# Reordering a sparse-attention stage: gates ahead of queries, alternating token tiles, and a delayed score step

## Chip, cores and metric

One core of a Trainium2 chip (trn2). The metric is the device time of one execution in microseconds (us); lower is better. The kernel is written by hand, one instruction stream for each engine: TensorE (PE, matmuls; PEld is its weight load), VectorE (DVE), ScalarE (ACT), GpSimd (POOL) and SyncE (SP, which only issues transfers). The streams meet at semaphores: `then_inc` raises one, `wait_ge` holds an engine's stream until it has reached a value.

## The reference

One layer of a decoder step for a prompt of 512 tokens and 8 samples of 8 new tokens (64 rows), all in float32, model width 1024:

```
h = rmsnorm(x);  z = h @ w_in           # hq hf hi hg | nq | kc vc ks vs kw vw | ngate | mgate
o_hg  = gated linear recurrence of 8 heads over hq, hf, hi, hg
o_nsa = g0 * compressed + g1 * selected + g2 * window     # 16 query heads, 4 kv heads of 64
u = sigmoid(mA) * o_hg + sigmoid(mB) * o_nsa;  x += rmsnorm(u @ w_out)
x += rmsnorm(conv_ffn(rmsnorm(x)))
```

The attention has three branches, each a softmax of its own, combined with a sigmoid gate per head and branch (`ngate`, 16 x 3 columns):

- compressed: means over blocks of 32 keys;
- selected: the 8 best blocks of 64 keys by the compressed probabilities (for the samples out of 4096 cached keys each, behind a page table); in the prompt of 512 tokens every causal block is selected;
- window: the last 512 keys.

The outputs are the new x, the new key and value rows of all branches, the window caches, the recurrence's states and the convolution's states.

## The kernel before

**Stages.** 0 to about 470 us: the norm of x and the recurrence, head by head, each with four products with 128 columns of `w_in`; beside it GpSimd gathers the compressed cache and DVE sums its blocks. To 547: the six key/value projections (blocks B_KV, units U_KV). To 571: transposes of the new keys (`kT`, units U_KT) and block means of the prompt (U_CM). To 635: eight query units (U_NQ), each 128 rows of queries for all 576 tokens. To 647: the gate unit (U_NG). To 857: the prompt's attention. To 1234: the samples' attention. Then merge gates, `w_out`, the FFN. The change touches 547 to 1234 us.

**Projection units** alternate between PSUM banks 0, 1 and 2, 3 (`2 * (u % 2)`); `banks_free(u)` waits until unit u - 2 has been copied away. Weights come in a ring of four slots on SP's queue (`weights(b)`, issued in order of b, L552). Before, the gate unit (L1936) runs behind the queries, with the tokens as the stationary operand: five token tiles by eight slices, 80 matmuls with 48 columns each. ScalarE takes the sigmoid of each tile (L958). Before `kT` is copied, ScalarE issues 13 transfers of new keys and values to the outputs (L940 to L944) on its own queue; its stream goes on to the copies of `kT` (L951, L952) behind them.

**The prompt's attention** is a list of 64 steps, `STEPS`, written out in this order: token tile i (0 to 3, 128 queries each), pair of kv heads gp, head r, branch br (selected or window). Step n does two heads (e = 0, 1) at once over (i + 1) * 128 keys. The engines work it in a pipeline:

- PE: `masked_scores(n)` (L1981, L1983) into banks 2 * (n % 2) and the next; transposes of the probabilities of step n - 2 (L2004); `values(n - 3)` (L1964, L1970).
- DVE: maximum of step n (L1425); reciprocal and scaling of head e = 0 of step n - 1 (L1430, L1433); copy of a transpose of step n - 2 (L1439); the output of every second step (L1411, L1412).
- ScalarE: exponential of step n (L979), copy of the other transpose (L989).
- GpSimd: scaling of head e = 1 (L747).

Every 16 steps, at the tile's end, the compressed branch of the next tile is done between the steps: `c_scores`, `c_exp`, `c_probs`, `c_transposes`, for all 16 heads of one tile. Ahead of its first scaling GpSimd issues 12 gathers of selected pages (`e_gather`, L736), which wait until the last projection unit is done, as their buffers lie in the weight ring.

**The samples' attention** is a loop of 96 steps. A sample has NC = 10 steps: c = 0 to 7 take four pages of 128 keys each, c = 8 the window of 512 keys, c = 9 the new rows. PE's step s:

- transposes the keys of step s: 8 transposes into banks 0 and 1 (L2091), one signal `ek_ok` behind both;
- transposes the probabilities of step m = s - LAG (L2099), LAG = 16, into banks 4 and 5 in turn;
- values of step m - 1 (`e_values`, L2055) into bank 6;
- scores of step s (L2116) from ScalarE's copy `kTs` of the transposed keys (L1034, both banks in one instruction);
- a piece of the block choice for the next sample: `e_c1` at c = 3, `e_c3` at 4, `e_c7` at 6, `e_c9` at 8.

DVE's step s waits for the scores of s, adds the block penalties (`penq`) and takes the maximum (L1525, L1528; L1530 to L1532 for the window); the block choice goes on in `e_c4`, `e_c6`, `e_c8` (L1465 to L1471), `e_c10` behind the scores of c = 4, 5, 7 and 9. ScalarE takes the exponentials of the last sample (`e_exp`, L1015) at c = 0 to 3, and DVE multiplies them with gate over sum (`e_scale`, L1483) at c = 4 to 6, before PE transposes them. Two merge gates (`gate0`) are computed in the loop's last steps.

Keys come in a ring of 6 buffers, loaded 4 steps ahead: of each four pages GpSimd gathers three (L736) and SP loads one (L592); all four pages of values are SP's, in a ring of 5. A window (L585) is one transfer. Both queues wait in program order: `ek_ok` frees a key buffer, `epv_ok` a value buffer.

Of the kernel before, what the change touches and what calls it, by code (L numbers as in the profile page):

```python
# [20 lines left out]
P = 128  # L21
D = 1024
T = 512
# [38 lines left out]
U_NQ = U_CM + 1  # L62
U_NG = U_NQ + 8
U_MG = U_NG + 1
# [3 lines left out]
B_NQ = B_KV + 6  # L68
B_NG = B_NQ + 4
B_MG = B_NG + 1  # L70
# [8 lines left out]
LAG = NC + 6  # L79
# [11 lines left out]
def build(nc, x_p, x_s, cache_c, cache_s, ptab, win_kv, st_hg, st_cv, w_in, lb_lg, hg_g, w_out, w_up,  # L91
# [3 lines left out]
    with ctx:  # L95
# [112 lines left out]
        pcm = view(NH * CB).rearrange("p (h c) -> p h c", c=CB)  # L208
        pcT = [view(T).rearrange("p (g t) -> p g t", t=P), avm.rearrange("p i r c -> p (i r c)").rearrange("p (g t) -> p g t", t=P)]
# [10 lines left out]
        kTs = [view(2 * PGC * P).rearrange("p (g n) -> p g n", g=2) for _ in range(2)]  # L220
# [8 lines left out]
        psm, psg, pscT = view(P), view(P), [view(P) for _ in range(2)]  # L229
# [101 lines left out]
        hgo_out = sem("hgo_out")  # L331
# [4 lines left out]
        qbd_ok = sem("qbd_ok")  # L336
        ge_ok = sem("ge_ok")
# [25 lines left out]
        eex_ok = sem("eex_ok")  # L363
        ecf_ok = sem("ecf_ok")
        epn_ok = sem("epn_ok")
# [13 lines left out]
        c10_ok = sem("c10_ok")  # L379
        pq_ok = sem("pq_ok")  # L380
# [26 lines left out]
        win_out = sem("win_out")  # L407
# [17 lines left out]
        def wcols(b):  # L425
# [6 lines left out]
            if b < B_NQ:  # L432
                o = O_KV + WB * (b - B_KV)
                return [(v, w_in3[:, :, o:o + WB])]
            if b < B_NG:
# [5 lines left out]
            if b < B_MG:  # L441
                return [(s[:, 0:KD * NH * BR].rearrange("p (k c) -> p k c", c=NH * BR),
                         w_in3[:, :, O_NG:O_NG + NH * BR])]
# [28 lines left out]
        def block_used(b):  # L472

            if b < B_KV:
                return proj, b + 1
            if b < B_NQ:
                return proj, U_KV + 5 * ((b - B_KV) // 2) + 5
            if b < B_NG:
                return proj, U_NQ + 2 * (b - B_NQ) + 2
            if b < B_MG:  # L480
                return proj, U_NG + 1
# [34 lines left out]
        obank = ps[:, 6, :]  # L516
# [4 lines left out]
        STEPS = [(i, gp, r, br) for i in range(PT) for gp in range(2) for r in range(R) for br in range(2)]  # L521
# [24 lines left out]
        def _(sp):  # L546
# [25 lines left out]

            sp.wait_ge(ge_ok, 1)
# [23 lines left out]
            sp.wait_ge(proj, U_NG + 1)  # L597
# [3 lines left out]
            sp.wait_ge(qbd_ok, 1)  # L601
            for s in range(NC * SB + LAG):
                b, c = divmod(s + KAHEAD, NC)
                if b < SB and c <= NPC:
                    kq = b * (NPC + 1) + c
                    if kq >= KAHEAD:
                        wait(sp, ek_ok, kq - NKR + 1)
# [7 lines left out]
                for n in range(NKR // 2):  # L615
                    if s == NC * SB - 3 + 2 * n:
                        sp.wait_ge(ek_ok, 1 * (SB * (NPC + 1) - NKR + 2 * n + 2))
# [24 lines left out]
            sp.wait_ge(hgo_out, 32 * HH)  # L642
            sp.wait_ge(win_out, 16 * SB)
# [1656 lines left out]
```

## Time and profile before

| | us |
|---|---|
| median of three runs (lowest, highest) | 1923.72 (1923.29, 1933.58) |
| the profiled execution | 1927.26 |
| its span, first to last instruction | 1925.5 |
| PE busy | 1758.1 (91%) |
| DVE busy | 955.7 (50%) |
| ACT busy | 522.3 (27%) |
| POOL busy | 625.2 (32%) |
| mean granted TensorE clock | 0.941 of full |

Busy PE includes the time that its matmuls take at a lower clock, so a busy PE need not be at its peak. The granted clock is given as a share of 2.4 GHz; 0.50 is 1.2 GHz. In the rows below, a bracket such as `[12.77 <-ACT mem L952]` is the engine's idle time before the instruction and what ended it; `x8` is the count of merged instructions.

### The profile page before, as it was taken

What the parts mean: (1) busy time and instruction counts of PE and PEld (TensorE: products, weight loads), DVE (VectorE), ACT (ScalarE), POOL (GpSimd) and SP (SyncE); (2) the same over time, 40 slices, a digit from 0 to 9 for tenths busy, and PEclk for the clock granted to TensorE, in tenths of its full rate; (3) what the DMA queues carried; (4) which work ended last, traced back from release to release, by engine and by line L of the source; (5) the groups of instructions that cost most, each with busy time, mean ns of one, the idle gap of its engine ahead of it and who ended that gap; (6) DMA issues with size and microseconds to landing.
All of it is one profiled execution on the core that took longest, in us unless ns stands there. A gap on an engine that the chain in (4) does not pass through costs nothing.

```text
span 1925.5 us, 25762 instructions
## 1 busy us (share of the span) xinstructions
PE 1758.1 (91%) x9675; PEld 1233.3 (64%) x9675; DVE 955.7 (50%) x1697; ACT 522.3 (27%) x1112; POOL 625.2 (32%) x630
## 2 busy tenths in 40 slices
PE   7999999999979799986788889998989999999996
PEld 6777777777857655653555556776467777763332
DVE  5776867772000257763445454233267777760003
ACT  3112221221110245542454445211222222320101
POOL 2334443341000222235455551231046565530000
PEclk9999999997979669997899999999989999999998
DMA  8676666654540100004677677452043232311211
GB/s 260 220 242 231 226 214 231 233 207 141 131 117 5 45 1 1 2 23 141 195 236 230 214 224 242 119 139 87 28 110 88 66 88 66 88 66 55 66 41 49
DMA packets 201014, 248.81 MB, mean 129 GB/s; under 512 B 32201, under 2 KB 173850, under 8 KB 192538
## 3 DMA queue, kind: packets, MB, share of 16 engines
q1 hardware_dynamic: 176684, 134.16, 23.9%
q0 software_dynamic: 21248, 109.46, 16.5%
q10 hardware_dynamic: 2960, 3.54, 0.5%
q8 instruction: 78, 1.28, 0.3%
q14 instruction: 44, 0.36, 0.1%
HBM read 236.09 MB, written 19.29 MB: 133 GB/s over the span
## 4 chain that ended last, share of the span: by engine, by line
PE 73%; DVE 11%; DMA 6%; issue 4%; ACT 3%; another core or an unknown queue 1%; ACTq 1%; SPq 1%; POOL 0%; DVEq 0%; POOLq 0%
PE ps L2142 20%; PE ps L2267 8%; PE ps L1743 6%; DVE mem L1253 5%; DMA mem<-in_cache_cmp_kv,pidx 5%; PE ps L2091 4%; PE ps L1754 4%; PE ps L2116 4%; PE ps L2206 3%; PE ps L1775 3%; PE ps L2055 3%; PE ps L1983 2%; PE ps L2004 2%; PE ps L1970 2%; ACT mem L1034 1%
## 5 line engine op out<-in xcount | busy, mean ns | idle before, releaser
L2142 PE MATMUL ps<-mem 128*128 128x288 f32 x1296 | 324.6, 408 | 0.8 <-DVE mem L1191 0.8
L736 POOL DMA_INDIRECT mem<-in_cache_sel_kv,sidx x192 | 186.0, 969 | 322.4 <-PE ps L1936 180.5
L2142 PEld LDWEIGHTS ps<-mem 128*128 128x128 f32 x1296 | 245.5, 191 | 67.7 <-DVE mem L1191 1.0
L1743 PE MATMUL ps<-mem 128*128 128x288 f32 x1024 | 270.1, 426 | 16.5 <-DVE mem L1279 15.4
L1743 PEld LDWEIGHTS ps<-mem 128*128 128x128 f32 x1024 | 203.7, 200 | 75.7 <-issue 16.4
L1253 DVE TENSOR_TENSOR mem<-mem 128x2048 f32<-128x2048 f32 x56 | 165.0, 2947 | 39.4 <-DMA mem<-in_cache_cmp_kv,pidx 38.9
L699 POOL DMA_INDIRECT mem<-in_cache_cmp_kv,pidx x56 | 88.4, 1579 | 242.4 <-DVE mem L1253 209.4
L2267 PE MATMUL ps<-mem 128*128 128x512 f32 x352 | 164.0, 609 | 0.0
L2116 PE MATMUL ps<-mem 128*64 128x512 f32 x288 | 82.0, 644 | 57.9 <-ACT mem L1034 33.8
L1525 DVE TENSOR_TENSOR mem<-ps,mem 128x512 f32<-128x512 f32 x64 | 44.2, 691 | 145.9 <-PE ps L2116 96.5
L2267 PEld LDWEIGHTS ps<-mem 128*128 128x128 f32 x352 | 64.0, 191 | 80.9 <-issue 80.5
L1034 ACT ACTIVATE mem<-ps 128x1024 f32<-128x1024 f32 x72 | 73.5, 1021 | 130.6 <-PE ps L2091 109.3
L2091 PEld LDWEIGHTS ps<-ident,mem 128*128 128x128 f32 x576 | 68.5, 151 | 41.2 <-issue 40.1
L1675 DVE SCALAR_TENSOR_TENSOR mem<-mem,cpar 128x592 f32<-128x592 f32 x88 | 93.3, 1081 | 1.6
L1754 PE MATMUL ps<-mem 128*128 128x256 f32 x384 | 88.9, 395 | 5.2 <-DVE mem L1279 5.2
L1687 DVE TENSOR_TENSOR st_ss<-st_ss 128x1 f32<-128x1 f32 (+1 forms) x5 | 0.8, 158 | 180.0 <-ACT mem L1153 179.9
L1754 PEld LDWEIGHTS ps<-mem 128*128 128x128 f32 x384 | 76.0, 199 | 17.6 <-DVE mem L1279 5.3
L2055 PE MATMUL ps<-mem 128*64 128x128 f32 (+1 forms) x1216 | 84.3, 278 | 2.1 <-DMA mem<-in_state_win_kv 1.1
L2091 PE MATMUL ps<-ident,mem 128*128 128x128 f32 x576 | 86.0, 297 | 0.0
L979 ACT ACTIVATE mem<-ps,nmx 128x128 f32<-128x128 f32 (+3 forms) x107 | 55.6, 524 | 103.4 <-DVE nmx L1425 100.8
L1775 PEld LDWEIGHTS ps<-mem 128*128 128x128 f32 (+1 forms) x640 | 73.3, 181 | 7.8 <-issue 6.7
L1425 DVE TENSOR_REDUCE nmx<-ps 128x2 f32<-128x256 f32 (+3 forms) x64 | 52.7, 824 | 47.3 <-PE ps L1983 46.7
(366 smaller groups left out, 2725.4 us busy)
## 6 DMA issues: line engine op xcount, KB each, us to landing
mem<-in_cache_sel_kv SPq DMA_DIRECT2D x320, 128.0 KB
mem<-in_w_up SPq DMA_DIRECT2D x44, 512.0 KB, 5.2
mem<-in_w_in SPq DMA_DIRECT2D x32, 512.0 KB, 7.3
mem<-in_w_in SPq DMA_DIRECT2D x14, 1024.0 KB, 5.9
mem<-in_w_down SPq DMA_DIRECT2D x10, 1024.0 KB, 5.0
mem<-in_state_win_kv SPq DMA_DIRECT2D x16, 512.0 KB
out<-in_state_win_kv POOLq DMA_DIRECT2D x8, 1008.0 KB, 15.8
mem<-in_x_prompt SPq DMA_DIRECT2D x8, 512.0 KB, 5.5
```

What stands on the lines that cost most here:

```text
L736: pool.indirect_dma_start(kring[kq % NKR][:, j, :], None, pool_rows, bass.IndirectOffsetOnAxis(sidx[:, i:i + 1], 0)).then_inc(pg_g[kq % NK ...
L1034: a.activation(kTs[kq % 2], ps[:, 0:2, :], ACT.Copy).then_inc(ekT_ok, 1)
L1253: ins = v.tensor_tensor(acc, acc, crot[u % 2], ALU.add)
L1675: ins = v.scalar_tensor_tensor(o, e, cpar[:, q, k:k + 1], o, ALU.mult, ALU.add)
L1743: mm = t.matmul(ps[:, 2 * (u % 2) + a, 0:NHF], lhs(k), hT[:, k, a * NHF:(a + 1) * NHF], start=(k == 0), stop=(k == KD - 1))
L1754: mm = t.matmul(ps[0:n, 2 * (u % 2) + a, 0:WB], hT[:, k, i * P:i * P + n], w[:, k, :], start=(k == 0), stop=(k == KD - 1))
L1775: mm = t.matmul(ps[0:n, 2 * (u % 2) + i // PT, (i % PT) * P:(i % PT + 1) * P], hT[:, j, i * P:i * P + n], wcol(b, 0)(j), start=(j == 0), s ...
L2055: mm = t.matmul(obank[gp * S:(gp + 1) * S, 0:P], pTs[m % 2][0:rows_in, j, gp * S:(gp + 1) * S], values, start=False, stop=(cc == NC - 1 an ...
L2091: mm = t.transpose(ps[:, gp, j * P:(j + 1) * P], kring[kq % NKR][:, j, gp * P:(gp + 1) * P], ident[:, :])
L2116: mm = t.matmul(out, qbd[:, b, gp, :], kTs[kq % 2][:, gp, :], start=True, stop=True)
L2142: mm = t.matmul(ps[:, bank, 0:NHF], lhs[:, k, :], rhs[:, k, :], start=(first and k == 0), stop=(k == KD // 2 - 1), skip_group_check=True)
L2267: mm = t.matmul(ps[:, bank, :], gT[:, k, i * P:i * P + n], ws[:, k - k0, :], start=(k == 0), stop=(k == NF - 1))
```

## The change

Five parts are changed together.

1. The 13 transfers of new keys and values are issued on SP's queue, behind the last weights of the queries, instead of ScalarE's.
2. The gate unit runs before the queries, with the weights as the stationary operand: 8 slices by two groups of tokens (256 and 320), the groups side by side in the array. ScalarE takes two sigmoids of it into `gsig` (a view of a buffer of the attention); five transposes (`gate_tokens`) bring it to token rows, DVE copies it to `gate`. The first compressed scores are done between query units 4 and 5, the first masked scores inside unit 7.
3. `STEPS` goes through the tiles in pairs, (3, 0) and then (2, 1): for each gp and r both branches of the first tile, then of the second. The compressed branch is done for two tiles and half of the heads at a time. The queries of the samples are laid out (`qbd`) in four portions between the steps.
4. In the samples, each of the two key banks has its own `ek_ok` and `ekT_ok` and its own copy; `kTs` has three buffers; the scores of step s - 1 are done in step s. The probabilities' transposes use bank 4 alone. LAG is 14. The block choice's parts move: `e_c5` and `e_c6` to c = 6, `e_c7` and `e_c8` to c = 8, `e_c9` to c = 9; `e_exp` to c = 1 to 4.
5. `e_scale` goes. Selected and window values are summed in two halves of a bank (5 and 6 in turn for successive samples) from unscaled exponentials, and `e_out` multiplies them by gate over sum when it copies them out. The compressed values have an accumulation of their own (`e_cv`, `e_cmp`).

GpSimd's window copies now wait for the recurrence's states to be out (one semaphore for both).

```diff
-LAG = NC + 6
+LAG = NC + 4
@@ steps of the prompt's attention
-        STEPS = [(i, gp, r, br) for i in range(PT) for gp in range(2) for r in range(R) for br in range(2)]
+        TILES = ((3, 0), (2, 1))
+        STEPS = [(i, gp, r, br) for ij in TILES for gp in range(2) for r in range(R) for i in ij for br in range(2)]
+        GPART = ((0, 0, 2 * P), (S, 2 * P, N - 2 * P))
@@ SP, behind weights(B_MG - 1); the same lines are taken out of ScalarE's stream
+            sp.wait_ge(kv_ok, U_KT - U_KV)
+            for k, (op, os) in enumerate(((cmp_p, cmp_s), (sel_p, sel_s), (win_p, None))):
+                c0 = 2 * KV * k
+                sp.dma_start(op[0, 0]..., kvt[:, 0:PT, c0:c0 + 2 * KV]).then_inc(kvo_out, 16)
...
@@ SP and GpSimd, key buffers
-                        wait(sp, ek_ok, kq - NKR + 1)
+                        wait(sp, ek_ok, 2 * (kq - NKR + 1))
@@ PE, gate unit (now before the queries)
-            for i in range(TT):
-                n = TR[i]
-                for k in range(KD):
-                    mm = t.matmul(ps[0:n, ...48 columns], hT[:, k, i * P:i * P + n], w[:, k, :], ...)
+            for k in range(KD):
+                for p0, o, n in GPART:
+                    mm = t.matmul(ps[p0:p0 + NH * BR, 2 * (U_NG % 2), 0:n], w[:, k, :], hT[:, k, o:o + n], ...)
@@ PE, queries
+            nq_unit(0)
+            gate_tokens()
+            for j in range(1, 5):
+                nq_unit(j)
+            pe.wait_ge(nq_ok, 4)
+            pe.wait_ge(cm_ok, 1)
+            c_scores(0)
+            nq_unit(5)
+            nq_unit(6)
+            nq_unit(7, first_scores)
@@ ScalarE, samples
-                    a.activation(kTs[kq % 2], ps[:, 0:2, :], ACT.Copy).then_inc(ekT_ok, 1)
+                    for gp in range(2):
+                        act.wait_ge(ek_ok, 2 * kq + gp + 1)
+                        a.activation(kTs[kq % 3][gp], ps[:, gp, :], ACT.Copy).then_inc(ekT_ok, 1)
@@ PE, samples
-                    wait(pe, ekT_ok, kq)
                     for gp in range(2):
+                        wait(pe, ekT_ok, 2 * kq + gp - 1)
...
-                    mm.then_inc(ek_ok, 1)
+                        mm.then_inc(ek_ok, 1)
...
-                if b < SB:
-                    (scores of step s)
+                if 0 < s <= NC * SB:
+                    scores(s - 1)
+                if b < SB and c == 1:
+                    e_cv(b)
...
-                    if c == 6:
+                    if c == 8:
                         e_c7(b + 1)
-                    if c == 8:
+                    if c == 9:
                         e_c9(b + 1)
@@ DVE, samples
-            def e_scale(b, pieces):
-                ...
+            def e_cmp(b):
+                dve.wait_ge(cv_ok, b + 1)
+                v.tensor_scalar(ocmp[b % 3], cbank[:, 256:384], gateq[:, b, 0:1], 1.0 / CB, ALU.mult, ALU.mult).then_inc(ocmp_ok, 1)
...
+                link(v.scalar_tensor_tensor(o, w[:, 0:P], est[:, b % 2, 20:21], o, ALU.mult, ALU.add))
+                    ins = v.scalar_tensor_tensor(osb[q, b, :], w[q, P + d:P + d + HD], est[q, b % 2, 21:22], o[q, d:d + HD], ALU.mult, ALU.add)
...
-                    if c == 7:
+                    if c == 8:
                         e_c8(b + 1)
```

## Rows read from the trace of the kernel before

**Rows 1.** The chain that ended last: start, length, what.

```profile
571.64 63.02 PE ps L1743 x256
634.66 12.02 PE ps L1936 x80
```

**Rows 2.** Timeline before the queries: start, length, engine, what.

```profile
553.35 7.52 ACTq L944 DMA_DIRECT2D out<-mem  x8
...
561.77 2.75 PE L1910 MATMUL ps<-ident,mem 128*128 128x128 f32 x10 [12.77 <-ACT mem L952]
```

**Rows 3.** Windows: length; PE, PEld, DVE, ACT, POOL busy; PEclk, DMA share, GB/s.

```profile
562.00:572.00 10.00, 10.00 (x36) 8.24 (x36) 0.24 (x2) 1.74 (x6) 0.00 (x0) 0.50 0.39 72
...
635.00:647.00 12.00, 11.66 (x77) 11.41 (x76) 2.48 (x17) 1.93 (x6) 0.06 (x1) 0.64 0.01 1
...
660.00:700.00 40.00, 34.57 (x189) 21.32 (x191) 18.25 (x68) 13.37 (x67) 8.66 (x16) 0.50 0.06 20
```

**Rows 4.** Timeline, start of the prompt's attention, GpSimd.

```profile
660.81 0.95 POOL L736 DMA_INDIRECT mem<-in_cache_sel_kv,sidx  x1 [0.30 <-issue]
661.79 0.46 POOL L747 TENSOR_SCALAR mem<-mem,ssm,gate 128x128 f32<-128x128 f32 x1
```

**Rows 5.** Timeline, PE: starts of every second step's scores, tiles 1 and 3.

```profile
725.41 0.28 PE L1981 MATMUL ps<-penb,identb 128*128 128x128 bf16 x2
...
729.91 0.29 PE L1981 MATMUL ps<-penb,identb 128*128 128x128 bf16 x2
...
822.31 0.28 PE L1981 MATMUL ps<-penb,identb 128*128 128x128 bf16 x2
...
829.28 0.28 PE L1981 MATMUL ps<-penb,identb 128*128 128x128 bf16 x2
```

**Rows 6.** Groups by form, attention: busy, mean ns; idle before.

```profile
L1425 DVE TENSOR_REDUCE nmx<-ps 128x2 f32<-128x1024 f32 x16 | 19.6, 1225 | 11.3 <-PE ps L1983 11.3
...
L747 POOL TENSOR_SCALAR mem<-mem,ssm,gate 128x512 f32<-128x512 f32 x11 | 11.4, 1038 | 24.9 <-DVE ssm L1430 24.9
```

**Rows 7.** Timeline, PE: attention's end, samples' steps 0, 14, 20, 70, two late steps, end.

```profile
854.58 1.92 PE L1970 MATMUL ps<-mem 128*64 128x128 f32 x32
...
863.83 1.97 PE L2091 MATMUL ps<-ident,mem 128*128 128x128 f32 x8
...
871.75 1.08 PE L2116 MATMUL ps<-mem 128*64 128x512 f32 x4 [1.11 <-ACT mem L1034]
...
922.85 1.92 PE L2091 MATMUL ps<-ident,mem 128*128 128x128 f32 x8
...
947.60 1.09 PE L2091 MATMUL ps<-ident,mem 128*128 128x128 f32 x8
...
1155.59 1.09 PE L2091 MATMUL ps<-ident,mem 128*128 128x128 f32 x8
...
1222.95 1.09 PE L2055 MATMUL ps<-mem 128*64 128x128 f32 x16
...
1224.56 1.09 PE L2055 MATMUL ps<-mem 128*64 128x128 f32 x16
...
1233.57 1.72 PE L2142 MATMUL ps<-mem 128*128 128x288 f32 x6
```

**Rows 8.** Windows, five samples' periods (columns as in Rows 3).

```profile
947.60:1155.60 208.00, 174.32 (x1614) 120.33 (x1611) 102.16 (x265) 103.15 (x176) 117.36 (x120) 0.99 0.75 229
```

**Rows 9.** Waits of SP's queue in the same 208 us: us, times, longest.

```profile
SPq L588 <- PE ps L2055: 26.1, 13, 7.6
SPq L588 <- remote: 23.0, 5, 7.3
```

**Rows 10.** Groups by form, samples' stage: GpSimd's gathers.

```profile
L736 POOL DMA_INDIRECT mem<-in_cache_sel_kv,sidx x176 | 170.7, 970 | 132.8 <-PE ps L2091 85.6 <-issue 39.0 <-remote 8.3
```

**Rows 11.** Timeline, DVE: first and last of `e_c8`'s instructions.

```profile
944.00 0.20 DVE L1466 COPY mem<-ps 32x63 f32<-32x63 f32 x1
...
945.11 0.18 DVE L1471 TENSOR_SCALAR mem<-mem 32x65 f32<-32x65 f32 x1
```

More of the change, by code:

```diff
@@ L970, in c_evac @@
                 a.activation(pcT[i % 2], ps[:, 7, :].rearrange("p (g t) -> p g t", t=P), ACT.Copy).then_inc(cpT_ok, 1)
-            c_exp(0)
+            for u in range(U_NQ, U_MG):
+                unit(u)
+                a.activation(halves(nqT[:, u - U_NQ, :]), pu(u), ACT.Copy, scale=SCALE).then_inc(nq_ok, 1)
+                if u == U_NQ + 5:
+                    c_exp(0)
             for n in range(NU + TLAG):
@@ L1922, in _ @@
             mm.then_inc(proj, 1)
-            for u in range(U_NQ, U_NG):
-                j = u - U_NQ
-                b = B_NQ + j // 2
-                if j % 2 == 0:
-                    weights(b)
-                feature(u, wcol(b, j % 2))
             banks_free(U_NG)
@@ new lines, in _, with nq_unit @@
+            mm.then_inc(proj, 1)
+            def nq_unit(j, ahead=None):
+                b, u = B_NQ + j // 2, U_NQ + j
+                if j % 2 == 0:
+                    weights(b)
+                lhs = wcol(b, j % 2)
+                banks_free(u)
+                for a in range(2):
+                    if a and ahead:
+                        ahead()
+                    for k in range(KD):
+                        mm = t.matmul(ps[:, 2 * (u % 2) + a, 0:NHF], lhs(k), hT[:, k, a * NHF:(a + 1) * NHF],
+                                      start=(k == 0), stop=(k == KD - 1))
+                mm.then_inc(proj, 1)
@@ new lines, in gate_tokens, with c_scores @@
+            def gate_tokens():
+                pe.wait_ge(gs_ok, 1)
+                for i in range(TT):
+                    x = int(i >= 2)
+                    p0, o, _ = GPART[x]
+                    src = gsig[p0:p0 + NH * BR, i * P - o:i * P - o + TR[i]]
+                    mm = t.transpose(ps[0:TR[i], 5 + x, i * NH * BR:(i + 1) * NH * BR], src, ident[p0:p0 + NH * BR, p0:p0 + NH * BR])
+                mm.then_inc(gt_ok, 1)
+            def c_scores(q):
+                tiles, gp = chain_parts(q)
+                if q:
+                    pe.wait_ge(cpT_ok, q)
+                for ii, i in enumerate(tiles):
+                    for r in range(R):
+                        j = ii * R + r
+                        mm = t.matmul(ps[:, 7, j * 2 * PB:(j + 1) * 2 * PB], nqT[:, gp * R + r, i * P:(i + 1) * P],
+                                      kcz[:, gp, :, :].rearrange("p e c -> p (e c)"), start=True, stop=True)
```

335 lines of the change are left out of this document (176 added, 159 removed).

## The prediction

> **What bounds the kernel now.** I read the chain of waits first. Nearly all of it is TensorE; the parts that the change can touch lie between 547 and 1234 us, and there the chain leaves PE often. I then went through this stretch in order of time.
>
> Before the queries, PE stands still for 12.77 us: ScalarE issues 13 stores of the new keys and values on its own queue (the last eight alone take 7.52 us) before it makes the copy that PE's transposes wait for [rows 2]. PE comes back at a granted clock of 0.50, its 1.2 GHz level, until 572 [rows 3]. The queries take 63.02 us, the gate unit behind them 12.02 us [rows 1], most of it at 1.2 GHz (0.64 in the mean) though PE is busy throughout [rows 3].
>
> The prompt's attention cannot start at the gate unit's end (646.7): GpSimd first issues 12 gathers, the last at 660.81, each 0.95 us and a gap of 0.30, and only then its first scaling, at 661.79 [rows 4]. PE moves on at 662.3. Tile 0 runs at 1.2 GHz [rows 3]; in later tiles PE is the bound: two steps (one branch each) repeat every 4.50 us in tile 1 and every 6.97 us in tile 3 [rows 5], with no gap on PE. It ends at 856.5 [rows 7].
>
> In the samples' stage a step begins with the transposes of the keys. Steps 0 to 13 take 59.0 us, 4.2 each, though the transposes take 1.09 us and the scores 1.08 at full clock [rows 7]: PE waits for ScalarE's copy of its transposes before it does the scores of the same step. Later ten steps (a sample) repeat every 41.6 us, from 947.60 to 1155.59 [rows 7]; PE is busy 174.3 of these 208 us, 34.9 per sample, DVE 102, ScalarE 103, the DMA engines 0.75 [rows 8]. The waits name the copy, hardly a transfer.
>
> **The change part by part**, against the profiled time of 1927.26 us (3.5 above the median of the three runs; span 1925.5).
>
> 1. The 13 stores go to SP's queue. SP has then issued the weights of the queries and has nothing due before the page loads, some 60 us later; the stores run beside the queries, and what waits for them (ScalarE and DVE, before the samples) is 230 us away. So the 12.77 us go. Behind them lie 9.2 us of PE work at 0.50 (561.8 to 571.0), which at full clock is some 5.2: -4. Part: **-16.8** (-12.8 if the clock falls all the same).
>
> 2. The gate unit goes ahead of the queries as 16 matmuls of 256 or 320 columns in place of 80 of 48. The nearest row is the queries' 256 matmuls of 288 columns in 63.02 us, 0.246 each [rows 1]: 4.0 us, against 12.0. On the path come five small transposes (0.8), the eight small matmuls of the compressed scores (1.9) and the first masked scores (1.3), which stood behind the last unit; and query unit 0 waits 0.9 us for DVE's copy. The queries' first 2 us no longer run at half clock (-1.2). Sigmoids, the softmax of the compressed scores and the gate copies lie beside 63 us of queries: nothing. Part: **-4.3** (-2 to -8).
>
> 3. GpSimd's 12 gathers still wait for the last unit, so the 15 us between that unit's end and the first scaling stay. What moved ahead of it only empties this wait: nothing gained, and PE idles some 11 us there.
>
> 4. Alternating tiles. The PE work is the same. By rows 5 a pair of steps grows by 1.24 us per tile, so 3.26, 4.50, 5.74 and 6.97; eight pairs of each are 163.8 us. I add 8 for the other compressed scores and their transposes, take off 3 (three steps' scores are done before the stall), and add 7 for the last steps' tail and for four rounds of small DVE instructions of the compressed softmax, partly beside PE (an estimate). New is the order 3, 3, 0, 0: the reciprocal of the first step of tile 3 stands on DVE behind the maximum of the second (1.23 us), then GpSimd scales for 1.04 [rows 6]. That is 2.6 us with hand-overs, and PE has only tile-0 work of 1.5 us and half of the transposes to put in front: some 0.7 per group of four, 5.6 in the first pair of tiles and 1.4 in the second. After the stall of part 3 PE restarts at 1.2 GHz; I add 4. Sum 186.8 against 194.2 (662.3 to 856.5): **-7.4** (+8 to -18, the end with no wait and no cold start).
>
> 5. Steps without values: 14 instead of 16, since the lag falls by 2. The keys go through two banks with a signal each, and the scores of a step are done in the next, so the copy's wait is off the path: 1.09 + 1.08 us and some 0.2 of the block-choosing chain, 2.4 per step. GpSimd needs 3 gathers of 1.28 us per page step [rows 10], 3.8, but is four steps ahead and has the window steps free: steps 10 to 13 are the first that it could hold up. 14 steps: 33, with 3 us of part 6's wait and 1.5 of cold start 37.5 against 59.0: **-21.5** (-10 if supply holds them, -26 at best).
>
> 6. Steps with values. DVE's scaling of all probabilities goes, replaced by a multiply-add on the small output; DVE is half idle here [rows 8], so by itself it is worth nothing. PE's floor is 34.9 us per sample. I see one new wait: the last matmul of the block choice stands on PE in step 9 right behind the scores of step 8, while DVE does its part only after it has taken in those same scores. That is 1.5 us for the window's scores, 1.3 for DVE's chain (944.00 to 945.29 [rows 11]) and 0.2 of hand-overs: 3.0 us of PE idle, with the next keys' transposes queued behind it. Period 34.9 + 3.0 + 0.4 = 38.3 against 41.6. Steps 14 to 19 come out at 23 against 24.7 (922.85 to 947.60), five samples save 16.5, the last sample, which has no block choice beside it, I leave as it is: **-18.3** (0 to -38).
>
> 7. Two steps fewer at the end, 1.61 us each [rows 7]: **-3.2**.
>
> Sum -71.5: 1927.3 - 71.5 = **1855.8 us**. From 1234 us on nothing changes.
>
> A page that speaks against part 4 is the Trainium skill's "TensorE: Matmul & The Clock Gate", section "HAM oscillation — how this bites in real kernels": an array that keeps pausing is throttled again and starts each burst at half rate. In the rows PE at 0.50 came back to full clock within about 10 us of dense work at 561 and 863, but not in tile 0, where it was busy too. By the rule the time would be that of the slower rival; by the rows I add 4 us.
>
> **The rivals.**
>
> *Supply becomes the bound in the samples* (1883 us). SP waited only 26.1 + 23.0 us of 208 [rows 9], so its issues take 31.8 us per sample; GpSimd's 24 gathers take 30.7; the DMA engines 0.75 of 41.6, 31.2. All lie a little below 38.3, and rings of five or six blocks must cover a bursty load. If landings grow late, the period stays at 41 and the first steps gain half: part 6 gives 1, part 5 gives 11: +27. For it: three supplies at 80% of the new period; against it: PE hardly waits for landings now. The Trainium skill's "DMA: Bandwidth & Descriptors", section "Specifications", gives about 358 GB/s of HBM per core. By that figure a sample's 9.5 MB (41.6 us at the row's 229 GB/s) would need 27 us, an estimate below all of these; no run here shows that rate for these loads.
>
> *Full overlap* (1831 us): the block-choice wait finds PE behind DVE, and the attention has no new waits: part 6 gains 15 more, part 4 10. For it: DVE is half idle; against it: both orders are written out.
>
> *Slower: the clock stays at 1.2 GHz through the attention.* Place: the restart at about 641 us, after 11 us of PE idleness, then uneven steps with a wait in each group of four. Price: eight transposes took 1.97 us at the low level and 1.09 at the high one [rows 7], a factor of 1.8 on 163.8 us, +131: **1983 us**. It decides once over 54% of the attention runs at that level. For it: tile 0, low for 40 us and more [rows 3]; against it: the clock rose as soon as tile 1's wider scores came, and tile 3's stand first now.
>
> *It does not do what it says*: SP issues the stores late and holds up the loads of pages and gate rows, and period and start stay. About 1922 us.
>
> **How the numbers follow.** Forecast 0.50, supply 0.22, full overlap 0.22, clock 0.04, no effect 0.02. The likeliest gives 1856; the range reaches from full overlap (1831) to supply (1883), rounded out by a microsecond: 1830 to 1884, which leaves out the last two cases and the tails. A measurement of this kernel can tell about 0.5% (10 us) from nothing: faster 0.94, same 0.02, slower 0.04.
>
> **What the profile after would show.** ScalarE queue: no stores between the last key/value copy and kT; queries from about 557. PE idle at 626 to 641 behind GpSimd's gathers. Group of four in tiles 3 and 0: 10.9 us. Step period 2.4 to 2.7 without values, sample period 38.3, with PE's wait before the block-choice matmul at 3 us, seven times. Wrong would be: a sample period at 41 with PE waiting for landings; a granted clock of 0.5 beyond some 10 us into the attention; no idle time at its start.

## The result and the profile after

The changed kernel takes 1905.68 us (median of 4 runs, 1903.52 to 1912.6), the kernel before beside it 1925.62 (4 runs): ratio 0.988, 95% interval 0.985 to 0.991. So it is faster, as forecast, but by 20 us (1.2%) and not by 71, and 1905.7 lies outside the range of 1830 to 1884. The profiled run, the slowest of the four, took 1912.6 us (span 1910.9, granted clock 0.950), 14.7 less than the profiled run before.

The part ahead of the samples came out nearly as forecast. The chain of waits of the changed kernel (start, length, what):

```profile
558.63 4.47 PE ps L1960 x29
...
571.36 31.24 PE ps L1974 x128
...
604.30 19.48 PE ps L1974 x80
...
643.29 0.95 POOL mem L762
...
838.47 3.69 PE ps L2176 x16
```

The gate unit (L1960) takes 4.5 us where it took 12.0 [rows 1], the queries run from 563 (before: 571.6), GpSimd's last of twelve gathers still stands ahead of its first scaling, now at 643.3 (before: 660.8 [rows 4]), and the samples' step 0 starts at 838.5 instead of 863.8 [rows 7], though the work ahead of the queries ended 2.5 us later this time.

From there the gain is lost again. One marker per sample makes this plain: TensorE's two transposes for the block choice of the next sample, in step 3 of each. In the kernel before they are L2015 and in the changed one L2077. Timeline, PE, before:

```profile
879.38 0.44 PE L2015 MATMUL ps<-ident,mem 128*128 128x128 f32 x2
...
922.37 0.69 PE L2015 MATMUL ps<-ident,mem 128*128 128x128 f32 x2
```

and after:

```profile
847.38 0.44 PE L2077 MATMUL ps<-ident,mem 128*128 128x128 f32 x2
...
891.18 0.69 PE L2077 MATMUL ps<-ident,mem 128*128 128x128 f32 x2
...
1073.43 0.44 PE L2077 MATMUL ps<-ident,mem 128*128 128x128 f32 x2
...
1118.10 0.44 PE L2077 MATMUL ps<-ident,mem 128*128 128x128 f32 x2
```

Up to the first marker the changed kernel is 32.0 us ahead. The next ten steps, in both kernels without values, take 43.8 us where they took 43.0: nothing of the forecast gain. The five samples from 891.18 to 1118.10 take 226.9 us, 45.4 each, where they took 207.1, 41.4 each: 19.8 us given back. The last four of them as windows (length; PE, PEld, DVE, ACT, POOL busy; PEclk, DMA share, GB/s), before and then after:

```profile
963.57:1129.48 165.91, 138.47 (x1290) 95.32 (x1289) 81.98 (x212) 82.60 (x140) 93.88 (x97) 1.00 0.75 229
```

```profile
937.69:1118.10 180.41, 148.69 (x1294) 104.08 (x1292) 69.94 (x192) 84.56 (x176) 90.87 (x97) 0.93 0.68 211
```

and TensorE's longest waits in them (us, times, longest), before:

```profile
PE ps L2116 <- issue: 16.1, 17, 1.8
PE ps L2116 <- ACT mem L1034: 10.5, 10, 1.5
```

and after:

```profile
PE ps L2093 <- DVE mem L1500: 13.3, 4, 3.8
PE ps L2176 <- issue: 5.8, 7, 1.2
```

The four samples are 14.5 us longer. TensorE's idle time is 31.7 us where it was 27.4: the waits for ScalarE's copy (10.5) have nearly gone, the waits for the choice of blocks (13.3) have come, and some 16 us that nothing in the profile ends ("issue") stand in both. Its busy time, for nearly the same number of matmul records, grew by 10.2 us, at a granted clock of 0.93 where it was 1.00.

Window of one such sample, to be read beside [rows 8]:

```profile
968.47:1013.25 44.78, 36.75 (x325) 25.27 (x324) 17.49 (x48) 21.10 (x44) 22.70 (x24) 0.96 0.67 209
```

And the end of that sample, timeline of VectorE and TensorE:

```profile
1009.88 0.17 DVE L1562 TENSOR_TENSOR mem<-ps,pen 128x8 f32<-128x8 f32 x1 [1.03 <-PE ps L2137]
...
1010.67 0.69 DVE L1564 TENSOR_REDUCE est<-mem 128x1 f32<-128x512 f32 x1
1011.28 0.21 DVE L1495 COPY mem<-ps 32x63 f32<-32x63 f32 x1
...
1012.39 0.18 DVE L1500 TENSOR_SCALAR mem<-mem 32x65 f32<-32x65 f32 x1
...
1012.63 0.69 PE L2093 MATMUL ps<-mem,rmatT 32*128 32x65 f32 x2 [3.34 <-DVE mem L1500]
...
1013.25 1.97 PE L2176 MATMUL ps<-ident,mem 128*128 128x128 f32 x8
```

This is the wait foreseen in part 6, in its place and nearly of its size: TensorE has issued the window's scores and stands still for 3.34 us while VectorE takes them in and then chooses the blocks. What was not foreseen is the last line: the clock has fallen behind the wait, and the next transposes take 1.97 us instead of 1.09.

Two theories had to be told apart. A: the wait for the choice, with the clock behind it, ate the gain. B: the key pages come too slowly on the way to step 0 of each sample, and the wait only hides that.

### The profile page after: what moved, and what is told of

Its sections match the earlier page's. It is cut to its first block, busy times and chain, and to the rows that moved or that the text cites. A ratio compares the mean times of both kernels' runs of the same rounds, so it can differ in the third digit from the quotient of the medians.

```text
span 1910.9 us, 25749 instructions
## 1 busy us (share of the span) xinstructions
PE 1748.1 (91%) x9640; PEld 1228.7 (64%) x9640; DVE 927.0 (49%) x1668; ACT 527.0 (28%) x1181; POOL 628.4 (33%) x630
## 4 chain that ended last, share of the span: by engine, by line
PE 72%; DVE 10%; DMA 5%; ACT 5%; issue 3%; another core or an unknown queue 3%; POOL 1%; DVEq 0%; SPq 0%; ACTq 0%; POOLq 0%
PE ps L2219 21%; PE ps L2344 8%; DMA mem<-in_cache_cmp_kv,pidx 5%; PE ps L1774 4%; PE ps L1785 4%; DVE mem L1270 4%; PE ps L2283 3%; PE ps L2124 3%; PE ps L1974 3%; PE ps L2176 3%; PE ps L1806 3%; PE ps L2137 2%; PE ps L2066 2%; PE ps L2020 2%
## 5 line engine op out<-in xcount | busy, mean ns | idle before, releaser
L2219 PE MATMUL ps<-mem 128*128 128x288 f32 x1296 | 324.6, 408 | 0.8 <-DVE mem L1208 0.8
L2219 PEld LDWEIGHTS ps<-mem 128*128 128x128 f32 x1296 | 245.5, 191 | 67.7 <-DVE mem L1208 1.0
L762 POOL DMA_INDIRECT mem<-in_cache_sel_kv,sidx x192 | 182.1, 949 | 319.5 <-PE ps L1974 157.1
L1774 PE MATMUL ps<-mem 128*128 128x288 f32 x768 | 210.2, 436 | 16.3 <-DVE mem L1296 15.3
L1774 PEld LDWEIGHTS ps<-mem 128*128 128x128 f32 x768 | 156.7, 206 | 62.8 <-issue 16.3
L1270 DVE TENSOR_TENSOR mem<-mem 128x2048 f32<-128x2048 f32 x56 | 157.8, 2817 | 44.2 <-DMA mem<-in_cache_cmp_kv,pidx 43.6
L2344 PEld LDWEIGHTS ps<-mem 128*128 128x128 f32 x352 | 64.0, 191 | 80.8 <-issue 80.7
L2124 PE MATMUL ps<-mem 128*64 128x128 f32 (+1 forms) x1216 | 90.7, 291 | 4.4 <-issue 4.4
L1785 PEld LDWEIGHTS ps<-mem 128*128 128x128 f32 x384 | 75.8, 198 | 17.1 <-DVE mem L1296 4.9
L2124 PEld LDWEIGHTS ps<-mem 128*64 128x64 f32 (+1 forms) x1216 | 69.7, 143 | 19.6 <-issue 18.7
L1051 ACT ACTIVATE mem<-ps 128x512 f32<-128x512 f32 x96 | 53.7, 597 | 103.2 <-PE ps L2176 62.1
L1806 PE MATMUL ps<-mem 128*128 128x128 f32 (+1 forms) x640 | 74.7, 275 | 0.0
```

The source lines that it names most:

```text
L762: pool.indirect_dma_start(kring[kq % NKR][:, j, :], None, pool_rows, bass.IndirectOffsetOnAxis(sidx[:, i:i + 1], 0)).then_inc(pg_g[kq % NK ...
L1270: ins = v.tensor_tensor(acc, acc, crot[u % 2], ALU.add)
L1774: mm = t.matmul(ps[:, 2 * (u % 2) + a, 0:NHF], lhs(k), hT[:, k, a * NHF:(a + 1) * NHF], start=(k == 0), stop=(k == KD - 1))
L1785: mm = t.matmul(ps[0:n, 2 * (u % 2) + a, 0:WB], hT[:, k, i * P:i * P + n], w[:, k, :], start=(k == 0), stop=(k == KD - 1))
L1806: mm = t.matmul(ps[0:n, 2 * (u % 2) + i // PT, (i % PT) * P:(i % PT + 1) * P], hT[:, j, i * P:i * P + n], wcol(b, 0)(j), start=(j == 0), s ...
L2124: mm = t.matmul(out[gp * S:(gp + 1) * S, br * P:(br + 1) * P], pTs[m % 2][0:rows_in, j, gp * S:(gp + 1) * S], values, start=False, stop=(c ...
```

## The experiments

All ratios are to the kernel before on the same chip. The first 16 kernels ran on chips where the kernel before takes 1877 to 1882 us, not 1925; only the last two met one like the first (1928). The marker is the same everywhere.

**The choice earlier, or later.** First, VectorE's `e_c8` ahead of the intake of the window's scores:

```
+                if b + 1 < SB and c == 8:
+                    e_c8(b + 1)
                 if s == NC * SB + 8:
...
-                    if c == 8:
-                        e_c8(b + 1)
```

> The changed kernel, but VectorE runs the choice of blocks of the next sample (max and match, 7 instructions) ahead of the intake of the window's scores, so that TensorE's ninth step no longer waits for it behind the scores issued just before. Theory A (this wait and the fall of the clock behind it ate the gain): the gap between the key transposes of step 8 and of the next sample's step 0 falls from 12.1 to about 7 us, the sample period from 44.8 to 39.5 us, seven times, so some 37 us less than the changed kernel: 1869 us. Theory B (the key and value pages arrive too slowly, and the wait only hides it): the period stays over 43 us and the time over 1893 us, with the transposes of the following steps waiting for transfers.

Second, TensorE's `e_c9` a step later instead:

```
+                if c == 0 and 0 < b < SB:
+                    e_c9(b)
                 if 0 < s <= NC * SB:
                     scores(s - 1)
...
-                    if c == 9:
-                        e_c9(b + 1)
```

> The changed kernel, but TensorE's product that spreads the choice (two matmul records, 0.7 us) stands one step later, in the next sample's step 0 behind its key transposes and values and ahead of scores(9); VectorE's order as changed. Theory A: the wait of 3.3 us is covered by a whole step of other matmuls, the clock stays up, 1869 us as in the first run. Theory B: over 1893 us.

Third, both:

> Both moves together. Theory A: nothing is left to gain by the second, 1865 to 1872 us. If the choice were still waited for in either of the first two (for instance because VectorE or ScalarE is late with the copy of the probabilities), this one alone is faster. Theory B: over 1893 us.

Measured: 0.967 (0.964 to 0.970), 0.968 (0.965 to 0.972) and 0.967 (0.964 to 0.970). All three are far below the changed kernel's ratio, and alike; the medians (1819.7, 1820.9, 1818.6) are lower than the forecasts because this chip is faster. The sample period (marker to marker) is 33.09, 33.6 and 33.20 us, steady from the third sample on. It could not be said yet how much of that was the chip, so the next two groups brought the unchanged kernels.

> The kernel before, unchanged, with a profile on the chip of this group. Both theories: ratio 1 within 0.3%. The profile is wanted for the sample period beside those of the other runs: if it is 41.6 us as in the first profile, chips differ elsewhere; if it is shorter, they differ in how fast the pages arrive.

> The changed kernel, unchanged, on the same chip. With the choice moved ahead of the intake the period was 33.2 us, with two gathers instead of three and the choice left where it is 37.6 us. Theory A (the wait for the choice and the clock behind it alone): the period here is 37 to 38 us as with two gathers, and the ratio to before 0.976 to 0.981. Theory B' (the wait and GpSimd's three gathers together: after the stall the pages of the next steps are late too): the period is above 41 us and the ratio 0.985 or more, as in the first measurement.

In a later group the changed kernel once more:

> The changed kernel again, on whichever chip this group gets. Both theories: if before takes 1880 us here, the period is 37.5 us and the ratio 0.981 to 0.985; if before takes 1925 us as in the first measurement, the period is 44 to 45 us and the ratio 0.985 to 0.990.

Measured: before 1.000 (0.998 to 1.002), changed 0.983 (0.979 to 0.988), and again 0.983 (0.979 to 0.986). The markers of the kernel before on such a chip:

```profile
873.22 0.44 PE L2015 MATMUL ps<-ident,mem 128*128 128x128 f32 x2
...
904.66 0.44 PE L2015 MATMUL ps<-ident,mem 128*128 128x128 f32 x2
...
977.20 0.44 PE L2015 MATMUL ps<-ident,mem 128*128 128x128 f32 x2
...
1012.85 0.33 PE L2015 MATMUL ps<-ident,mem 128*128 128x128 f32 x1
```

and of the changed one:

```profile
850.08 0.44 PE L2077 MATMUL ps<-ident,mem 128*128 128x128 f32 x2
...
874.89 0.33 PE L2077 MATMUL ps<-ident,mem 128*128 128x128 f32 x1
...
950.67 0.44 PE L2077 MATMUL ps<-ident,mem 128*128 128x128 f32 x2
...
988.16 0.44 PE L2077 MATMUL ps<-ident,mem 128*128 128x128 f32 x2
```

The period is 35.65 us before and 37.49 after, and the ten early steps go from 31.4 to 24.8. The changed kernel's period is that of theory A, 37 to 38 us, and not over 41 as theory B' had it; its ratio lies a little above the 0.976 to 0.981 of A. Moving the choice is thus worth 28 us on such chips (1819.7 against 1848.1), where 37 were forecast. Chips differ mostly in this stage (the kernel before reaches the queries 2 us earlier and has a similar attention, then its samples are 6 us shorter each), and on both kinds the changed period is the longer one, by 1.8 us here and by about 4 on the first. A window of one sample of the changed kernel and, second, of the one with the choice ahead:

```profile
936.35:973.84 37.49, 34.69 (x325) 25.12 (x324) 17.58 (x48) 20.91 (x44) 22.65 (x24) 0.95 0.83 253
```

```profile
930.37:963.46 33.09, 33.09 (x325) 23.75 (x324) 17.58 (x49) 20.89 (x44) 24.43 (x26) 1.00 0.95 299
```

With the choice ahead TensorE is busy all of the time at a granted clock of 1.00. The difference of 4.40 us is 2.80 us of waiting and 1.60 us by which the same 325 matmul records became longer at a clock of 0.95. The wait is there in every sample, the lower clock in most. One of the changed kernel's samples kept 1.00 behind the same wait of 2.80 us and took 2.80 us more than 33.17, no more:

```profile
988.16:1024.13 35.97, 33.17 (x326) 23.76 (x324) 17.59 (x48) 20.91 (x44) 22.67 (x25) 1.00 0.87 266
```

The wait itself, on PE's timeline of the changed kernel, and the same place with the choice ahead:

```profile
973.48 0.43 PE L2093 MATMUL ps<-mem,rmatT 32*128 32x65 f32 x2 [2.80 <-DVE mem L1500]
973.84 1.09 PE L2176 MATMUL ps<-ident,mem 128*128 128x128 f32 x8
...
977.74 1.49 PE L2176 MATMUL ps<-ident,mem 128*128 128x128 f32 x8
```

```profile
963.10 0.43 PE L2093 MATMUL ps<-mem,rmatT 32*128 32x65 f32 x2
...
963.21 0.17 DVE L1564 TENSOR_TENSOR mem<-ps,pen 128x8 f32<-128x8 f32 x1 [0.33 <-PE ps L2137]
...
963.46 1.09 PE L2176 MATMUL ps<-ident,mem 128*128 128x128 f32 x8
```

In the second the product waits for nothing, and VectorE takes in the window's scores behind it. The Trainium skill's "TensorE: Matmul & The Clock Gate", section "HAM oscillation — how this bites in real kernels", describes such a cost: pauses between bursts of matmuls, there for transfers, throttle the array again, and the next burst starts cold, at half rate. The runs agree in the main: without the pause the clock stayed at 1.00, with it most samples lost 1.6 us. They differ in that the drop came only behind the first transposes (1.09 us at 973.84, then 1.49 at 977.74) and was missing in the sample at 988.16.

**The choice made longer.** The search for the maxima twelve times in place of once:

```
+                for _ in range(12):
-                link(v.max(out=est[0:q, 0, 24:32], in_=imp[0:q, :]))
+                    link(v.max(out=est[0:q, 0, 24:32], in_=imp[0:q, :]))
```

> The changed kernel with the search for the maxima in the choice of blocks done twelve times instead of once (11 more of 0.22 us and their links, some 2.7 us more on VectorE each sample). Theory A: the choice is on TensorE's path for all of its length, so the sample period grows by 2.7 us or more, the more by what a longer rest costs in clock: 7 times 2.7, at least 19 us, ratio 0.993 or more. If the wait were hidden behind late pages (theory B), the period grows by under 1 us and the ratio is at most 0.987.

Measured 0.996 (0.994 to 0.999), period 40.6 to 40.9 us, 3.3 us more per sample. TensorE's wait grew from 2.80 to 5.55 us, by as much as the eleven searches take (0.25 us each from start to start):

```profile
978.50 0.68 PE L2094 MATMUL ps<-mem,rmatT 32*128 32x65 f32 x2 [5.55 <-DVE mem L1501]
```

The choice is on the path for all of its length. Theory A holds on these chips.

**GpSimd's share.** Two pages of four gathered in place of three, with the choice as changed, then ahead:

```
-K_POOL = (0, 1, 2)
+K_POOL = (0, 1)
```

> The changed kernel with two of the four key pages of a step gathered by GpSimd instead of three (2.5 us of issue per step instead of 3.7), and two loaded by SyncE. Theory A: the wait for the choice is untouched, the time stays at 1906 us within 6 us, or grows as SyncE's queue becomes later. Theory B with GpSimd as the narrow place: the waits at the start of each step shrink and the time falls by over 10 us, below 1896 us.

> The choice ahead of the intake and two gathers instead of three. Theory A and B' both: with the wait gone TensorE is the bound, the period stays at 33.2 us, and the ratio is the 0.967 of the run with three gathers, within 0.4%. If the pages still cost something there, it is under 0.963.

Measured 0.979 (0.975 to 0.982), period 37.58, and 0.969 (0.966 to 0.973), period 33.09 once and then 34.3 to 34.8. The first misses theory A's "1906 within 6 us", which was written for another chip, and its period decides: 37.58 with two gathers, 37.49 with three. What it gains it gains earlier, since eight gathers and not twelve stand ahead of the prompt's attention. In the second this gain is spent again: from 923 to 1027 us TensorE waits three times, 4.0 us in all, for a sample's window, which SyncE issues, most likely because SyncE has more to issue.

**The start of the attention.** The choice ahead, and the first pages by SyncE alone:

```
             for kq in range(KAHEAD):
-                e_load(kq, 0, K_SP)
+                e_load(kq, 0, list(range(PGC)))
...
-            pool.wait_ge(proj, U_MG)
-            for kq in range(KAHEAD):
-                e_gather(kq)
```

> The choice ahead of the intake (0.967 of before), and the key pages of the first four steps loaded by SyncE, four a step, so that GpSimd issues no twelve gathers before its first scaling in the prompt's attention. If GpSimd's queue holds up that start, as the prediction had it, the gap at the first attention steps (11 to 12 us) closes and the run is 8 to 12 us faster than with the choice ahead alone: ratio 0.961 to 0.963. If something else holds up the start (the chain for the first samples, the gate), the ratio stays at 0.967.

Measured 0.962 (0.958 to 0.966), 1808.2 us. In the changed kernel TensorE waits for GpSimd's first scaling, here GpSimd scales at once:

```profile
647.49 1.12 PE L2066 MATMUL ps<-ident,mem 128*128 128x128 f32 x4 [11.26 <-POOL mem L773]
```

```profile
633.35 1.03 POOL L770 TENSOR_SCALAR mem<-mem,ssm,gate 128x512 f32<-128x512 f32 x1 [161.79 <-DVE ssm L1455]
```

So part 3 named the cause rightly. From the start of the last key/value unit to the samples' step 0 this kernel takes 282.3 us (544.39 to 826.72), the run with only the choice moved 294.7 (546.02 to 840.75): 12.4 less. It is the fastest kernel of the study. The ratios differ by 0.5%, some 9 us, and their intervals overlap; the stretch in the traces is the clearer evidence.

**The parts of the first half.** First the old samples' stage behind the new first half: the change taken back in every function of the samples (the lag, the two banks, the order of the scores, the scaling), of which these are the core:

```
-LAG = NC + 4
+LAG = NC + 6
...
-                if 0 < s <= NC * SB:
-                    scores(s - 1)
...
+                if 4 <= c < 7 and 0 < b <= SB:
+                    e_scale(b - 1, ([0, 1], [2, 3], [4])[c - 4])
```

> The changed kernel up to the end of the prompt's attention (stores on SyncE, gate ahead, alternating tiles), but the samples' stage of the kernel before (scores in the same step, scaling on VectorE, one bank). By the account of the prediction the first part is worth 28 us and the samples' stage of before 370 us: ratio 0.985, about 1855 us where before takes 1882. If theory A or B' holds, the changed kernel's samples' stage is worth nothing or less, and this run is as fast as the changed kernel or faster by up to 12 us; if it is slower than the changed kernel, the scores a step behind pay for their wait on this chip.

Then no alternation:

```
-        STEPS = [... for r in range(R) for i in ij for br in range(2)]
+        STEPS = [... for i in ij for r in range(R) for br in range(2)]
```

> The changed kernel, but within a group of the attention all steps of the first tile, then all of the second, instead of alternating; the chains of the compressed branch stay grouped as changed. The prediction gave the alternation and its pairing 7.4 us. If that holds, the ratio is 0.987 where the changed kernel has 0.983; if the alternation does nothing, 0.983 within 0.3%.

And the stores back on ScalarE:

```
-            sp.wait_ge(kv_ok, U_KT - U_KV)
-                sp.dma_start(op[0, 0]...
...
+            act.wait_ge(kv_ok, U_KT - U_KV)
+                act.dma_start(op[0, 0]...
```

> The changed kernel, but the 13 stores of keys and values are issued by ScalarE ahead of its copies of the transposed keys, as in the kernel before. The prediction gave the move to SyncE 16.8 us: the ratio then is 0.992 where the changed kernel has 0.983. Should the gate unit, which now stands ahead of the queries, give TensorE work meanwhile, less: 0.988 or under.

Measured 0.987 (0.981 to 0.992), 0.982 (0.978 to 0.986) and 0.989 (0.985 to 0.993). The new first half alone is worth 1.3% here, some 25 us, and the new samples' stage beside it 0.4% (0.983 against 0.987), which its interval cannot tell from nothing; with the choice ahead it is worth 2%. The stores' place is worth 0.6% by the ratios, 11 us. In the trace the wait is back nearly whole:

```profile
558.63 2.75 PE L1941 MATMUL ps<-ident,mem 128*128 128x128 f32 x10 [12.39 <-ACT mem L969]
```

and from the start of the last key/value unit to the start of the gate unit the run takes 28.4 us (540.05 to 568.44) against 13.9 (546.02 to 559.87) in the changed kernel: 14.5 us, near the 16.8 forecast.

The alternation by itself is worth nothing that can be measured. The attention from TensorE's first transposes behind GpSimd's gathers to the samples' step 0, as windows of the kernel before, the changed one and the one without alternation:

```profile
662.31:863.83 201.52, 183.75 (x1525) 117.59 (x1525) 139.41 (x359) 95.52 (x323) 54.83 (x69) 0.87 0.03 8
```

```profile
645.12:838.40 193.28, 168.84 (x1522) 111.05 (x1522) 139.73 (x377) 92.25 (x317) 53.97 (x69) 0.97 0.02 6
```

```profile
645.02:839.16 194.14, 176.35 (x1522) 113.63 (x1522) 138.44 (x377) 92.13 (x317) 53.97 (x69) 0.90 0.02 6
```

The changed attention is 8.2 us shorter on the first chip (6.0 on a fast one, 198.9 against 192.9), and it is so without the alternation too. With it TensorE works at a higher clock but waits more (idle 24.4 us against 17.8), and the two cancel. This run keeps the pairs of tiles, the widest tile first and the compressed branch by halves, so the gain must come from these; which of them brings it was not tested.

**The slower chip.** Why were the first chip's periods 41.4 and 45.4 us? Additional transfers, from memory to memory, on SyncE's queue:

```
+                if what == 0 and kq >= KAHEAD:
+                    sp.dma_start(spare_d[kq], pool_rows[0:2 * P, :]...[:, 0, :])
```

> The changed kernel with one more 128 KB copy from memory to memory on SyncE's queue for each of the 60 later groups of key pages (11% more to move; it computes the same). Theory C (the first chip's longer periods are pages that come later, so load on the DMA engines does the same elsewhere): the period grows from 37.5 us to over 41 us and the time by over 25 us. Theory D (the first chip is slow in something else, the load does nothing while its share is under 0.9): within 1.5 us of 37.5, the time within 12 us of the changed kernel.

> The kernel before with the same additional copies. Theory C: the period grows from 35.65 us by less than in the changed kernel, since only 6.9 us of it, not 10, are spent at steps 8 and 9: 37 to 40 us, ratio 1.005 to 1.017. Theory D: 1.000 to 1.005.

> The changed kernel with the choice ahead of the intake (period 33.1 us with the DMA engines busy for 0.91 to 0.95 of it) and the additional copies. Theory C and D both: 11% more to move in 33.1 us would be a share over 1.0, so the transfers become the bound, the period 35 to 38 us, ratio 0.974 to 0.983. If it stays at 33.1 us, the share of busy time doesn't tell how near that bound is.

Measured 0.983 (0.978 to 0.987), 1.001 (0.999 to 1.003) and 0.972 (0.969 to 0.974), periods 37.57, 35.65 and 33.09: not one of them moved, as theory D has it for the first two. The third was a miss for both theories: a DMA share of 0.97 is no bound yet. Then pages asked for two steps ahead in place of four, in both kernels:

```
-KAHEAD, VAHEAD = 4, 4
+KAHEAD, VAHEAD = 2, 4
```

> The changed kernel with the key pages asked for two steps ahead instead of four (and six gathers instead of twelve ahead of the prompt's attention, worth some 6 us at its start). Theory C (late pages, the first chip's case): pages land later than their step begins, waits without a local releaser appear at the key transposes as in the first chip's profile, the period grows from 37.5 us to over 41. Theory D (pages land in under two steps here): the period stays within 1.5 us of 37.5 and the start is 6 us earlier, ratio 0.980.

> The kernel before with the same. Theory C: the period grows from 35.65 us to 39 or more, less than in the changed kernel or the same, since its steps are the slower ones (4.0 against 3.45 us) and give the pages more time. Theory D: 35.65 us, ratio 0.995 to 0.998 from the start.

These two met a chip of the slow kind. Measured 0.992 (0.990 to 0.994) and 1.006 (1.004 to 1.009), against 0.988 and 1 unchanged. So the forecasts by period (37.5, 35.65), made for the faster chips, don't apply; beside the first two profiles the changed kernel's periods are 43.2 to 47.0 us (unchanged: 44.5 to 46.5) and those of the kernel before 43.6 to 47.4 (unchanged: 41.2 to 41.8). The ten early steps take 42.5 and 43.5 us. So on slow chips these ten steps take 42.5 to 43.8 in four kernels, whether a step's work on TensorE is short or long and whether pages are asked for two or four steps ahead; on the others they take 20.9 (both moves of the choice) to 31.4 (before). If the latency of a page set the pace, one would expect half the lead to lengthen these steps much; they didn't grow. This looks like a rate at which pages arrive, which no run here isolates. It is not the DMA engines' load, whose share is lower on the slow chip (changed kernel, the ten early steps, first chip and then a fast one):

```profile
847.40:891.20 43.80, 29.07 (x134) 14.71 (x132) 15.55 (x39) 14.53 (x28) 24.26 (x27) 0.75 0.52 163
```

```profile
850.10:874.90 24.80, 21.86 (x134) 12.48 (x132) 15.61 (x39) 13.18 (x26) 18.91 (x20) 0.93 0.72 215
```

Waits of ScalarE that nothing on the core ends appear in the profiles of slow chips alone (changed kernel on the first chip; us, times, longest, 220 us of the samples):

```profile
ACT mem L1051 <- remote: 25.9, 11, 3.5
ACT avm L1051 <- remote: 21.3, 8, 3.9
```

The same view of the changed kernel on a faster chip has none. Which part of the path of a page is slow there stays open. The versions with the choice ahead and with two gathers never met such a chip, and that would be the next run.

## Why the prediction was wrong

- **Part 1, stores**: right. The wait of 12.77 us went; from the start of the last key/value unit to the first matmul behind the transposes and block means the stretch fell from 28.6 to 13.3 us, 15.4 of the 16.8 forecast, and the undone move gives back 14.5.
- **Part 2, gate**: the unit takes 4.5 us, by the step's sum 4.0. From there to TensorE's restart in the attention 4.3 us are gained, as said, but only on the first chip: there the old gate unit ran mostly at the lower clock (0.64 in the mean) [rows 3]. In the second profile of the kernel before it took 9.3 us and not 12.0 (631 to 641 us: 0.88), and the gain is 0.1 us.
- **Part 3**: right, the start waits 11.3 us for GpSimd, and the run that took the gathers away shows the cause.
- **Part 4, alternation**: the number is right (8.2 us to the samples' step 0, forecast 7.4), the name is not. From TensorE's restart to the last value matmul the attention takes 186.2 us (645.1 to 831.3), forecast 186.8; the new waits came (idle time up by 6.7 us, forecast 7.0), and the low clock of tile 0 went (660 to 700 us: 0.50 before [rows 3], 1.00 after). But without the alternation it is as fast.
- **Part 5, steps without values**: forecast 21.5 us. On the first chip steps 0 to 13 took 53.2 us (838.47 to 891.66) against 59.0: 5.8, all of it in the first three. On a fast chip they fell from 49.0 to 34.8: 14.2. The step that failed is the reading behind [rows 7] and [rows 8], "the waits name the copy, hardly a transfer". On the first chip the ten early steps took 43 us in either kernel, so another pace stood behind the copy's wait, most likely the pages'; and in the later samples more of TensorE's waits name nothing (16.1 us) than name the copy (10.5), which the prediction passed over.
- **Part 6, steps with values**, is the step that cost the most: "Period 34.9 + 3.0 + 0.4 = 38.3 against 41.6". The wait was foreseen and its price about right (2.80 to 3.83 against 3.0). Left out was the clock behind it, 1.6 us in most samples. And all 6.7 us of idle time in the old period were counted as freed. The floor itself, 34.9, was too high: with no wait, on a fast chip, the sample took 33.09. On the fast chips the old period had only 2.1 us of idle time (33.57 busy of 35.65), so the wait and its clock turn a possible gain of 2.6 into a loss of 1.8: 33.1 + 2.8 + 1.6 = 37.5. On the first chip both periods are 6 to 8 us longer, 41.4 and 45.4, and the same exchange shows: in four samples the copy's 10.5 us of waits give way to 13.3 for the choice, the 16 us that name nothing stay, and the lower clock adds 10.2 us of busy time.
- **The sum.** In the first two profiles parts 1 to 4 brought 25.4 us of 28.5 (27.9 if the 2.5 us later start of the trace after is taken off), part 5 5.8 of 21.5, and parts 6 and 7 a loss of 16.5 in place of a gain of 21.5 (from step 14 to the end 1004.4 us before, 1020.9 after). The miss of 56.8 us is 3.1 + 15.7 + 38.0.
- **Part 7**: behind the last marker the changed kernel is 3.3 us shorter (794.5 against 797.8), but only 2.2 of it lie before the end of the samples' stage (101.9 against 104.1); that it comes to the 3.2 forecast is luck in part.
- **The rivals.** No single one held: supply, the nearest, was priced with the new wait hidden under it, and both added up instead. The clock was feared at the attention's start, where it was up (a mean of 1.00 between 660 and 700 us), and fell at the samples' ends.

The direction was right, since the first half's gain didn't hang on any of this. What keeps the change from bringing more is, on the fast chips, the place of one group of small instructions: moved ahead, the same change is worth 3.3% instead of 1.7%. What moving it would bring on the first kind of chip was not measured.

## What to carry to other kernels

When scores or other results are taken in a step later, look at every small chain that ends on the late engine: an instruction that needs nothing from the intake must not stand behind it. A foreseen wait can cost more than its length when the clock falls behind it, here 4.4 us for 2.8 in most samples. A rewritten order needs its parts undone one by one: here the alternation, named in the title, did nothing that could be measured. And idle time may be counted as freed only if the row that fills it has been named: a stretch with little work that still takes as long as one with much (43.0 us for ten steps without values, 41.4 for ten with them) suggests that something outside the engines sets the pace.

## What the runs showed of the hardware

Chips of one kind differ by 2.5% on the same program (1877 to 1882 and 1925 to 1928 us for the kernel before), and most of the difference lies in the stage that gathers pages by index: 35.65 against 41.4 us a sample, with the DMA share at 0.87 and 0.75 over four of them. Of the 53.9 us between the two traces of the kernel before, 44.7 lie in the samples' stage, 7.9 ahead of it (step 0 at 863.8 and 856.0) and 1.3 behind.

The DMA engines took 11% more transfers, at a share of 0.95 before, and the sample period stayed at 33.09 us; they moved 311 GB/s with a share of 0.97:

```profile
950.00:1050.00 100.00, 98.90 (x967) 70.96 (x965) 52.38 (x142) 62.69 (x132) 68.89 (x74) 1.00 0.97 311
```

A rest of TensorE of 2.80 us at the end of each sample was mostly followed by matmuls at the lower level of 1.2 GHz for a part of the next one or two steps, and the mean clock of the sample was then 0.95 instead of 1.00. Behind some rests of the same length it did not fall: once in the changed kernel on a fast chip, and in two of five samples on a slow one (pages asked for two steps ahead).
